# Key products and bonus products moved from a stage of their own into the decay loop of one projection stage

## The reference

```
def rwkv_inputs(u, conv_w, w0, w2, a0, a2, k_k, k_a):
    r, k, v = split(conv1d_centred(u[..., :3 * RWKV_W], conv_w))
    decay = exp(-exp(-softplus(-w_lora) - 0.5))
    a = sigmoid(a0 + einsum("btdr,drc->btdc", ad, a2))
    kk = normalised per head (k * k_k)
    kd = k[:, :, None] * (1 + (a - 1) * k_a)          # one per direction

def step(s, inp):                                     # the recurrence, later
    sa = s @ kk_t
    s = s * w_t - outer(sa, kk_t * a_t) + outer(v_t, k_t)
    y = s @ r_t

# in rwkv_output: one bonus for both directions
bonus = einsum("bthn,btdhn,hn->bth", rh, kdh, r_k)[..., None] * vh
```

## Time and profile before

| | us |
|---|---|
| three runs | 1966.37, 1969.11, 1975.32 (median 1969.11) |
| the profiled execution | 1969.11 |
| its span in the trace | 1967.2 |
| PE busy in the span | 1788.9 (91%) |
| DVE busy | 979.7 (50%) |
| ACT busy | 391.1 (20%) |
| POOL busy | 175.3 (9%) |

### The profile page before, as it was taken

The page is one execution under the profiler, slowest core; times in us unless marked ns, Lnnn a source line. Parts: engine busy times, 40 slices in busy tenths (PEclk is TensorE's granted clock), DMA queues, the critical chain, the costliest instruction groups (busy, mean ns, idle before and its releaser), DMA issues. The chain is left out here.

```text
span 1967.2 us, 27838 instructions
## 1 busy us (share of the span) xinstructions
PE 1788.9 (91%) x11842; PEld 1053.2 (54%) x11842; DVE 979.7 (50%) x1613; ACT 391.1 (20%) x715; POOL 175.3 (9%) x226
## 2 busy tenths in 40 slices
PE   7999987879999999999999999899979889888876
PEld 3544577764444444488887888664453223333322
DVE  1773874553389888862289788643050010100013
ACT  4223542432110101100121111540031000000001
POOL 0000217610000000000010111100000000000000
PEclk9999997999999999999998999999979899889899
DMA  8462033114321212412377332302539999999995
GB/s 346 164 246 75 16 86 93 45 19 169 129 84 66 85 65 86 158 68 89 128 264 252 118 97 86 134 1 96 251 153 408 426 426 426 427 425 427 425 426 235
DMA packets 78753, 379.67 MB, mean 193 GB/s; under 512 B 34225, under 2 KB 37297, under 8 KB 52385
## 3 DMA queue, kind: packets, MB, share of 16 engines
q1 hardware_dynamic: 68768, 349.83, 45.9%
q0 software_dynamic: 7104, 26.68, 3.7%
q10 hardware_dynamic: 2752, 1.31, 0.2%
HBM read 363.83 MB, written 19.92 MB: 195 GB/s over the span
## 5 line engine op out<-in xcount | busy, mean ns | idle before, releaser
L3360 PE MATMUL psum<-mem 128*64 128x512 f32 x1504 | 354.7, 627 | 41.4 <-DMA mem<-in_w_upe 21.6
L2083 PE MATMUL psum<-mem 128*128 128x512 f32 x704 | 302.9, 591 | 0.6 <-ACT mem L379 0.6
L3360 PEld LDWEIGHTS psum<-mem 128*64 128x64 f32 x1504 | 116.8, 144 | 258.5 <-issue 254.0
L2192 DVE SCALAR_TENSOR_TENSOR mem<-mem 128x512 f32<-128x512 f32 x352 | 237.0, 747 | 0.0
L2083 PEld LDWEIGHTS psum<-mem 128*128 128x128 f32 x704 | 132.9, 189 | 170.2 <-issue 169.0
L2434 PE MATMUL psum<-mem 128*128 128x256 f32 x896 | 199.3, 384 | 5.5 <-DVE mem L2615 4.9
L2434 PEld LDWEIGHTS psum<-mem 128*128 128x128 f32 x896 | 171.4, 192 | 33.3 <-DVE mem L2615 4.6
L1614 PE MATMUL psum<-mem 128*128 128x256 f32 x616 | 136.8, 382 | 2.9 <-DVE mem L1596 1.6
L3422 DVE TENSOR_TENSOR mem<-mem,psum 128x512 f32<-128x512 f32 x16 | 11.0, 688 | 256.1 <-issue 225.5
L1614 PEld LDWEIGHTS psum<-mem 128*128 128x128 f32 x616 | 116.3, 190 | 22.1 <-issue 5.4
L706 PE MATMUL psum<-mem 128*128 128x512 f32 (+1 forms) x336 | 119.0, 513 | 0.0
(11 more groups left out here) (397 smaller groups left out, 2223.9 us busy)
## 6 DMA issues: line engine op xcount, KB each, us to landing
mem<-in_w_upe SPq DMA_DIRECT2D x31, 2048.0 KB, 28.3
mem<-in_w_gate SPq DMA_DIRECT2D x30, 2048.0 KB, 30.8
mem<-in_w_downe SPq DMA_DIRECT2D x29, 2048.0 KB, 32.7
mem<-in_ada SPq DMA_DIRECT2D x32, 1024.0 KB, 6.3
mem<-in_w_up SPq DMA_DIRECT2D x22, 1024.0 KB, 4.8
mem<-in_ada POOLq DMA_DIRECT2D x16, 1024.0 KB, 6.1
mem<-in_w_in_g SPq DMA_DIRECT2D x12, 1024.0 KB, 5.0
mem<-in_w_down SPq DMA_DIRECT2D x16, 704.0 KB, 4.4
```

The source lines that it names most:

```text
L2083: last = pe.matmul(k.bank[2 * (m % 3) + h2][:, :], w[:, kt, h2], h[:, kt], start=kt == 0, stop=kt == KD - 1)
L2192: ins = dve.scalar_tensor_tensor(out=a, in0=src, scalar=w, in1=a, op0=MUL, op1=ADD)
L3360: last = pe.matmul(bank[halves[h], :], xs[:, kt, halves[h]], pair[h][0][:, kt, cols], start=kt == 0, stop=kt == tiles - 1, skip_group_chec ...
```

## The change

Seven edits, all in this stage:

1. DVE's first loop (kd and a · kk for all units) is gone. Both products are made inside the decay loop, in a temporary (`kd[n % 2]`) for kd, and K is written from it.
2. ACT makes the scaled copy 1 + (a - 1) · k_a inside the decay loop, behind the two Exps of its unit.
3. POOL does nothing here any more. DVE makes r_k · kd · r for each unit and direction, 8 SCALAR_TENSOR_TENSOR of 128x512, in one buffer (`prod`).
4. PE has 8 bonus matmuls, two per ct summed in PSUM, with the unscaled head matrix; ACT's scaling of that matrix is gone.
5. PE's order: two of the eight `fourier` parts stand among the rates, before four did.
6. The one-element Exp ahead of ACT's loop is gone.
7. Two places in memory change sides: `late_w` is now written in rows of 512 with a pitch of 768, and the sums of another small product lie elsewhere; a wait on DVE that guarded the old place is gone.

The diff, without the lines on names and places that repeat this:

```
-    late_w = late_weights.rearrange("p (j w) -> p j w", j=KD)
+    late_w = late_weights.rearrange("p (j w) -> p j w", j=KD)[:, :, 0:CH]
...
-            pool.wait_ge(s["kk"], KC)
-            pool.wait_ge(s["conv"], n_conv)
-            for ct in range(KC):
-                pool.wait_ge(s["kd"], 2 * ct + 2)
-                pool.tensor_tensor(prods[ct], K[:, 0, ct, CTX:ALL], in_time(1, K[:, 1, ct, CTX:ALL]), ADD).then_inc(s["both"], 1)
-                pool.wait_ge(s["both"], ct + 1)
-                pool.tensor_tensor(prods[ct], prods[ct], r[:, ct], MUL).then_inc(s["prod"], 1)
...
-            def bonus(ct):
-                pe.wait_ge(s["heads"], ct + 1)
-                pe.wait_ge(s["prod"], ct + 1)
-                if ct >= 2:
+            def bonus(n):
+                ct, d = units[n]
+                pe.wait_ge(s["prod"], n + 1)
+                if ct >= 2 and d == 0:
                     pe.wait_ge(s["bonus"], ct - 1)
-                pe.matmul(k.bank[6 + ct % 2][:, :], heads[:, ct], prods[ct], start=True, stop=True,
+                pe.matmul(k.bank[6 + ct % 2][:, :], k.c("head_ones"), prod, start=d == 0, stop=d == 1,
...
-            for ct in range(KC):
-                if ct:
-                    rates(ct)
-                fourier(ct)
+            fourier(0)
+            rates(1)
+            fourier(1)
+            rates(2)
+            rates(3)
             pe.wait_ge(s["a"], 8)
...
-                if n < 4:
-                    fourier(n + 4)
-                if n in (1, 2, 4, 5):
-                    bonus((1, 2, 4, 5).index(n))
+                if n < 6:
+                    fourier(n + 2)
+                bonus(n)
...
-                act.wait_ge(s["a"], 2 * ct + 2)
-                for d in range(2):
-                    act.activation(K[:, d, ct], B[:, d, ct], ACT.Identity, bias=omka[:, ct:ct + 1], scale=k.v("k_a", ct)).then_inc(s["scale"], 1)
...
-                act.activation(heads[:, ct], k.c("head_ones"), ACT.Identity, scale=k.v("r_k", ct)).then_inc(s["heads"], 1)
-            act.activation(k.small[:, 62:63], k.v("zero"), ACT.Exp).then_inc(s["warm"], 1)
...
                 act.activation(e_inv[n % 2], sums, ACT.Exp, scale=-DECAY_SCALE).then_inc(s["e_inv"], 1)
+                act.activation(kd[n % 2], B[:, d, ct], ACT.Identity, bias=omka[:, ct:ct + 1], scale=k.v("k_a", ct)).then_inc(s["scale"], 1)
...
-            for n, (ct, d) in enumerate(units):
-                dve.wait_ge(s["scale"], n + 1)
-                for x in stretches(d):
-                    ins = dve.tensor_tensor(K[:, d, ct, x], K[:, d, ct, x], in_time(d, kf[:, ct, x]), MUL)
-                ins.then_inc(s["kd"], 1)
-                for x in stretches(d):
-                    ins = dve.tensor_tensor(B[:, d, ct, x], B[:, d, ct, x], in_time(d, kk[:, ct, x]), MUL)
-                ins.then_inc(s["kk_a"], 1)
-            dve.wait_ge(s["kk_a"], 8)
...
-                dve.wait_ge(s["both"], ct + 1)
+                dve.wait_ge(s["scale"], n + 1)
+                for x in stretches(d):
+                    ins = dve.tensor_tensor(t2[:, x], t2[:, x], in_time(d, kf[:, ct, x]), MUL)
+                ins.then_inc(s["kd"], 1)
+                for x in stretches(d):
+                    ins = dve.tensor_tensor(B[:, d, ct, x], B[:, d, ct, x], in_time(d, kk[:, ct, x]), MUL)
+                ins.then_inc(s["kk_a"], 1)
+                dve.wait_ge(s["kd"], n + 1)
+                if n:
+                    dve.wait_ge(s["bonus_mm"], n)
+                dve.scalar_tensor_tensor(out=prod, in0=in_time(d, t2[:, CTX:ALL]), scalar=k.v("r_k", ct), in1=r[:, ct],
+                                         op0=MUL, op1=MUL).then_inc(s["prod"], 1)
                 dve.wait_ge(s["e_inv"], n + 1)
-                dve.tensor_tensor(K[:, d, ct], K[:, d, ct], e_inv[n % 2], MUL).then_inc(s["k_done"], 1)
+                dve.tensor_tensor(K[:, d, ct], t2, e_inv[n % 2], MUL).then_inc(s["k_done"], 1)
+                dve.wait_ge(s["kk_a"], n + 1)
                 dve.tensor_tensor(B[:, d, ct], B[:, d, ct], e_inv[n % 2], MUL).then_inc(s["b_done"], 1)
-                if n in (2, 4, 5, 6):
-                    dve.wait_ge(s["a_done"], n)
-                    bonus((2, 4, 5, 6).index(n))
+                if d == 0 and ct:
+                    bonus(ct - 1)
+            bonus(KC - 1)
```

More of the change, by code:

```diff
@@ L626, in first_projection_stage @@
     fourier_in = ring(4096, 2048).rearrange("p (c t) -> p c t", c=KC)
-    upto0, inv_at, prods, heads_at = temps
-    heads = heads_at.rearrange("p (c m) -> p c m", c=KC)
+    upto0, inv_at, scaled0, scaled1, prod = temps
     squares = inv_at.rearrange("p (n w) -> p n w", n=2)
-    root, inverse = prods[0][:, 0:W4], prods[0][:, W4:2 * W4]
+    root, inverse = prod[:, 0:W4], prod[:, W4:2 * W4]
     e_upto = [x.rearrange("p (c t) -> p c t", t=CHUNK + 1) for x in (upto0, ring(6144, 780))]
     e_inv = [inv_at[:, ALL * i:ALL * i + ALL] for i in range(2)]
+    kd = [scaled0, scaled1]
     omka = k.small[:, 0:4]
-    late_w = late_weights.rearrange("p (j w) -> p j w", j=KD)
+    late_w = late_weights.rearrange("p (j w) -> p j w", j=KD)[:, :, 0:CH]
     chunks = lambda x: x.rearrange("p (c t) -> p c t", t=CHUNK)
@@ L646, in first_projection_stage @@
         "one_minus", "raw", "square", "length", "root", "inverse", "spread", "kk", "sig_mm", "sig", "a_mm", "a", "ones", "sum",
-        "e_upto", "decay", "e_inv", "scale", "a_done", "r_done", "kd", "both", "prod", "heads", "warm", "k_done", "kk_a", "b_done", "bonus_mm", "bonus")}
+        "e_upto", "decay", "e_inv", "scale", "a_done", "r_done", "kd", "prod", "k_done", "kk_a", "b_done", "bonus_mm", "bonus")}
     mod_step = [k.sem("first_mod_step"), 0]
@@ L864, in _ @@
             act.wait_ge(s["mod_turned"], 1)
-            act.wait_ge(s["one_minus"], 1)
             for ct in range(KC):
                 take_rates(ct)
-                act.activation(heads[:, ct], k.c("head_ones"), ACT.Identity, scale=k.v("r_k", ct)).then_inc(s["heads"], 1)
-            act.activation(k.small[:, 62:63], k.v("zero"), ACT.Exp).then_inc(s["warm"], 1)
+            act.wait_ge(s["one_minus"], 1)
             act.wait_ge(s["ones"], 2)
@@ L887, in bonus @@
             def bonus(ct):
-                dve.wait_ge(s["bonus_mm"], ct + 1)
+                dve.wait_ge(s["bonus_mm"], 2 * ct + 2)
                 dve.tensor_tensor(bonus_v[:, ct], k.bank[6 + ct % 2][:, :], vf[:, ct, CTX:ALL], MUL).then_inc(s["bonus"], 1)
@@ L896, in _ @@
             for i, m in enumerate(order):
-                if i == 7:
-                    dve.wait_ge(s["conv"], 8)
                 for j in range(slots, slots + (2 if i == 7 else 1)):
@@ L928, in _ @@
             for n, (ct, d) in enumerate(units):
-                dve.wait_ge(s["scale"], n + 1)
-                for x in stretches(d):
-                    ins = dve.tensor_tensor(K[:, d, ct, x], K[:, d, ct, x], in_time(d, kf[:, ct, x]), MUL)
-                ins.then_inc(s["kd"], 1)
-                for x in stretches(d):
-                    ins = dve.tensor_tensor(B[:, d, ct, x], B[:, d, ct, x], in_time(d, kk[:, ct, x]), MUL)
-                ins.then_inc(s["kk_a"], 1)
-            dve.wait_ge(s["kk_a"], 8)
-            for n, (ct, d) in enumerate(units):
+                t2 = kd[n % 2]
                 dve.wait_ge(s["e_upto"], n + 1)
@@ L2281, in block_one @@
     r_stored = k.sem("scan_r_stored")
-    temps = (k.at(28672, 780), k.at(34048, 2 * ALL), [k.at(40704, SEQ), k.at(31744, SEQ), k.at(30208, SEQ), k.at(30976, SEQ)], k.at(33536, 4 * P))
-    first_projection_stage(k, start, norm1, h, u, zeros, convs, (lora, w0_rows), (k.at(10240, 4096), k.at(20520, 512)),
-                           A, R, K, B, r, kf, kk, vf, bonus_v, chunk_decay, wd, ad, k.at(6144, 4096), r_dram, r_stored, temps)
+    temps = (k.at(28672, 780), k.at(34048, 2 * ALL), k.at(31744, ALL), k.at(30208, ALL), k.at(40704, SEQ))
+    first_projection_stage(k, start, norm1, h, u, zeros, convs, (lora, w0_rows), (k.at(6144, 4096), k.at(20520, 512)),
+                           A, R, K, B, r, kf, kk, vf, bonus_v, chunk_decay, wd, ad, k.at(10240, 6144), r_dram, r_stored, temps)
     context_of = lambda at: three(at, 8, ALL)[:, :, 0:CTX]
```

## The result

| | before | after |
|---|---|---|
| median, us | 1967.63 (10 runs, 1961.38 to 1975.32) | 1980.58 (10 runs, 1973.68 to 1990.16) |
| span of the profiled execution | 1967.2 | 1986.8 |
| PE's first rates to its first matmul of the recurrence ("the stage") | 58.61 | 70.03 |
| from there to the end of the span ("behind") | 1713.0 | 1722.9 |

The ratio is 1.0062, with a 95% interval of 1.0043 to 1.0083: slower, as forecast, by 12.9 us of the medians where 10.6 was forecast. The interval is clear of 1, but its lower end is under the 0.5% that the prediction counted as a change. The forecast time was 1979.7.

The account below looks back on a forecast made before the run. The prediction took the end of DVE's list to set the stage's end: the decay loop grows by 15.9 us and starts 5.3 earlier, so 1969.1 + 10.6 = 1979.7 us, range 1973 to 1986.

Parts of the forecast that it names:

- Start of the decay loop: DVE's decay loop, waiting for the first Exp, starts at 216.33 us instead of 221.59, 5.3 us earlier.
- Length: DVE's decay loop, now with kd, a · kk and bonus products, takes 48.2 us instead of 32.3, 15.9 more.
- The stage: DVE's decay loop ends 10.6 us later, at 264.5 us, and the whole kernel shifts by as much.
- PE is a little faster, and it is ahead: In the decay loop PE needs 5.5 us per unit against DVE's 5.6 to 6.0, so DVE is not held up.
- The clock inside the loop: Rival, chance 0.07: PE's clock falls before the decay loop and stays down, PE bounds it; 10 to 15 us lost, about 1992.
- The end of DVE's list sets the end of this stage: Before the barrier DVE's last product ends at 253.89 us, PE starts the recurrence at 254.22; shifts pass on in full.
- DVE is quicker: Rival, chance 0.06: the 0.865 us rows still hold a loss to POOL; 5.4 us go from 48, time 1974.
- The clock behind the barrier: Rival, chance 0.11: the half-clock stretch from 310 to 330 us runs at full clock, 7.9 us back, time 1971.8.
- Signs of being wrong: Wrong if DVE waits for PE inside the loop, or the part behind the barrier is not 1713.0 us as before.

Follow-up runs that it names:

- a_warm: The changed kernel with the one-element Exp put back ahead of ACT's decay loop; stage 68.74 us, median 1976.66 us, ratio 1.0056.
- a_no_product: The changed kernel without DVE's eight bonus products, the bonus matmuls multiplying r itself; stage 65.73 us, median 1974.19 us, ratio 1.0044.
- a_no_bonus: The changed kernel without the eight bonus products and without the eight bonus matmuls; stage 64.20 us, median 2045.35 us with more experts' matmuls run.
- b_no_pool: The kernel before without POOL's eight products, the bonus matmuls multiplying r itself; stage 58.61 us, median 1966.28 us, ratio 1.0004.
- b_sums_early: The kernel before with some summed logs earlier in PE's list, bonus matmuls re-placed, DVE's last bonus product behind unit 7; stage 57.08 us, ratio 0.9986.
- b_dve_bonus: The kernel before with eight bonus products on DVE in the decay loop, eight bonus matmuls, POOL idle; stage 62.02 us, ratio 1.0018.
- a_fourier4: The changed kernel with PE's old order, four early fourier parts among the rates; stage 73.36 us, median 1985.39 us, ratio 1.0083.
- after_again: The changed kernel profiled and measured once more without edit; stage 70.03 us, behind the barrier 1713.3 us, median 1980.56 us, ratio 1.0058.

## Why the prediction was right

- *Start of the decay loop.* Forecast 216.33 - 195.61 = 20.72 us behind the first rates, measured 20.99. The chain (four rates, sigmoids, summed logs, load, Exp) is as written, the load's 1.28 in it shown by a_warm. The hops up to the load were 0.08 us longer in sum; most of the rest is the last one. From the end of the Exp to DVE's first product it took 0.20 us (214.63 to 214.83) where I put 0.03. Why, no run shows.
- *Length.* Forecast 48.2, measured 48.72. The bonus product took 0.67, kd and a · kk 0.87 and 0.94, as priced from rows of other lines; kd of the first unit did not wait for ACT. The missing half microsecond is mostly the 0.43 us wait for the last bonus matmul. I had PE wait for DVE there and the matmul take about half a microsecond; it took 2.08 at half clock. At the 1.02 that it takes elsewhere it would have ended at 261.76 by my estimate, ahead of DVE's 262.34, and there would have been no wait. It is the only wait in DVE's loop, and so all that the clock cost there.
- *The stage.* Forecast +10.6, measured +11.42. That the whole moved by 12.9 us of the medians, and 13.0 the second time, leaves about 1.5 us over the stage, well inside the intervals of some 4 us to either side. That the forecast time, 1979.7, lies only 0.9 us from the median is in part luck: it started from 1969.1, where ten runs have a median of 1967.63, and the shift was 2.3 us too small; the two errors cancel in part.
- *"PE is a little faster, and it is ahead."* Right in result, wrong in margin. I gave PE 5.5 us per unit with half a microsecond for the bonus matmul, but a 128x512 matmul counts 2 of the 8 of a `fourier` row, so by that row it was 0.9, and the trace of before had its own row with 1.02. PE needs 5.64 against DVE's 5.6 to 6.2 (the longest with a product from PSUM). bonus(0) and bonus(1) were to be done 2.8 and 3.3 us before DVE wanted their buffer; both were done 0.9 us before (222.95 against 223.86, 228.58 against 229.47). a_no_product shows how thin that is: take 5.3 us of DVE's work away and 4.3 come back, the rest only when the bonus matmuls go too (a_no_bonus).
- *The clock inside the loop.* This rival's first half happened: the clock was at half from 216 to 219 and PE lost 0.8 us at the summed logs and 0.9 at the fourier part, which its lead covered, with the 0.9 us to spare that stand above. It came back, so nothing was late.
- *"The end of DVE's list sets the end of this stage."* True of the end, not of the middle of the kernel before. b_no_pool took all of POOL's contention away, 7.6 us of DVE's time by my count and 7.3 by the rows of the two profiles, and the stage did not move. 3.4 us of it reached the decay loop (2.47 by an earlier start, 0.96 by a quicker first A) and went in waits for Exps that wait for PE; the rest had already gone in the first loop, where DVE waited 4.1 us for ACT's scaled copies instead of 0.35. b_sums_early, where PE's order differs (and the place of DVE's last product with PSUM), shows the same from the other side. My sum didn't use it, since I took the old loop as measured; but the rival "DVE is quicker" was priced on the wrong idea that DVE's gains always show: of 5.3 us of DVE's work, a_no_product gave back 4.3.
- *The shares.* They depend on the order in which the parts are taken. Added to the kernel before, the bonus on DVE and PE costs 3.41 us (b_dve_bonus) and the rest 8.01. Taken out of the changed kernel, the bonus gives back 70.03 - 64.20 = 5.83 (a_no_bonus), and the rest costs 64.20 - 58.61 = 5.59 over b_no_pool, the kernel before without the bonus products. The sum is 11.42 either way: what a part costs depends on whether DVE's waits for Exps take it up. In the rest stand the load (1.29, a_warm) and PE's new order (3.33 the other way, a_fourier4), so giving up the loop ahead is worth about 8.01 - 1.29 + 3.33 = 10.05 us with the bonus in place and 5.59 - 1.29 + 3.33 = 7.63 without it. These were not measured one on top of another, and no run moves that loop alone, so both figures are worked out, not shown.
- *The clock behind the barrier.* As a rival it stood for the other sign. What the runs show is that this part differs by up to 11 us between executions of like code. So one profile can't tell a change of 10 us in this kernel by its span; the marks can.
- *Signs of being wrong.* Both that I named came up. DVE did wait for PE inside the loop, 0.43 us where I allowed 0.2, and the part behind the barrier was 1722.9 in the first profile, not 1713.0. The first is the half microsecond above. The second was a badly chosen sign, as after_again shows: it can come up without any change.

## What to carry to other kernels

Work that needs no result of a slow chain is best done while the chain runs: eight units of kd and a · kk ran beside PE's rates and cost some 8 to 10 us behind them, as worked out above. Before pricing what a slow neighbour costs an engine, look for its next wait: b_no_pool had gained 3.4 us by the end of the decay loop's first product and lost it all in later waits. In a kernel whose far part wanders by more than the change is worth, measure between two marks of the trace that stand around the change, and take the time of the whole only as a check.

## What the runs showed of the hardware

PE's clock at half showed in single rows: the summed logs of one unit took 2.39 us instead of 1.60 (clock 0.50 during a part of it), a bonus matmul 2.08 instead of 1.02 (0.50 throughout, after 5.29 us without work on PE). DVE waited 0.43 us for that one matmul, so a matmul that comes seldom can cost the engine behind it at the lower clock's price. A table load behind a wait was paid in full (1.29 us between a_warm and the changed kernel), and no drain was seen beside it. Beside POOL's products an a · kk on DVE took 1.91 us instead of 1.03 and an A 1.92 instead of 0.96, and the stage was no longer for it.
